# First layer's output projections in three terms for 14 of 16 tiles, one modulation group moved, VectorE's order changed in the first layer

## The chip, the cores and the metric

The kernel runs on one core of a Trainium2 chip. The metric is the device time of one execution in microseconds (us). TensorE multiplies matrices, VectorE and ScalarE do elementwise work, GpSimd (POOL) does masks and some transfers, SyncE (SP) issues most of the weight loads.

## The reference, cut to what matters

Two models of two layers each run one after the other on 256 tokens of width 1024. Only the first layer of the first model is touched by the change:

```python
cond = jax.nn.silu(c)
mod = cond @ ada_w[l] + ada_b[l]
shift, scale, gate = jnp.split(mod, 3, axis=-1)
h = rms_norm(x, norm_g[l]) * (1.0 + scale[:, None, :]) + shift[:, None, :]
z = h @ even_w_in[j]
a_val, a_glu, a_gate, r, k, v, wd, ad, b_gate = split_cols(z, EVEN_SIZES)
ya = conformer_conv(a_val, a_glu, conv_w[j], conv_vec[j]) * jax.nn.silu(a_gate)
yb = rwkv7_mix(r, k, v, wd, ad, ...).astype(h.dtype)
yb = yb * jax.nn.silu(b_gate)
out = jnp.concatenate([ya, yb], axis=-1) @ even_w_out[j]
x = x + gate[:, None, :] * out
```

`conformer_conv` is a causal convolution of 31 taps per channel with a layer norm; `rwkv7_mix` is a recurrence over heads of 64 channels with a norm per head. All is float32.

## The kernel before, in words

The activations lie transposed: 8 tiles (KT) of 128 channels by 256 tokens. Each engine has one hand-written program, and its order is the order of the code; engines wait for each other on counting semaphores. A queue of loads on SP fills a ring of weight slots, each as soon as its last reader is done (`place`, and L2486 where SP waits).

**The head.** The modulation `mod` is made in groups of 512 columns. `ada(c, half)` on VectorE multiplies four weight rows by `cond` and adds them up (L3152, L3156); `ada(c)` on TensorE sums over the partitions with one-column matmuls (L2605). The first four groups are made before hT, the normed input, can be scaled (L3200) and shifted by ScalarE (L2958). TensorE fills its waits with `keep_busy`, matmuls of ones whose result is not used (L2597). `AUX` holds constants for ScalarE's evictions.

**The projections of the first layer.** `z` (L2620) makes one tile of 128 output channels: eight float32 matmuls of 256 columns, one for each k. The trace has two records for each float32 matmul. VectorE takes keys, receptances and values with `lerp` (L3205) after ScalarE has thinned them (L2971). The keys' stage ends with L3275 and L3277, whose semaphore rwkv_set lets TensorE make head pairs (`lt_pair`, L2641).

**Masks and taps.** The convolution's 248 taps (`conv(n)`, L3226) are handed out on VectorE between other work. In the second half of the tokens they stand beside `kar_masks` and `br_masks` (L3325), which take head products from banks 2 and 3 so that TensorE can write the next pair there (`br_pair`, L2685). `states` then runs four steps of the recurrence.

**The output projections.** `eoA` are 8 tiles that multiply YY, the convolution branch, and `eoB` 8 tiles that multiply YT, the recurrence branch. VectorE adds each tile times the gate into xT (`out`, L3423). eoA tiles alternate between two banks: tile q waits for the sum of tile q-2. eoB uses four banks and begins when all eoA tiles are summed. Between the eoA tiles lies the norm over heads of YT: its sums and spreads on TensorE (L2457, L2467), squares and root on ScalarE (L3121, L3123), centring (L3441), reciprocal and scaling (L3450) on VectorE, gain and bias on ScalarE (L3126), then bonus and gate on VectorE (L3454, L3455). Behind eoB comes the second layer's norm (index 1), whose squares ScalarE makes as tiles are summed. VectorE also makes `ada(10)` between the halves and `ada(11)` after the norm, and the angle tables between the eoB sums.

The second layer's q projections (L746, code in `pe_rest`) already work in three terms: ScalarE copies a weight chunk of 256 columns in fp32r (`hb_r`, L1379), VectorE writes the rest, weight minus copy, over the chunk in the ring (L1753), and TensorE adds high times high, high times low and low times high.

## Time and profile before

| what | us |
|---|---|
| median of 3 runs | 2012.23 (2012.07 to 2014.06) |
| the profiled execution | 2008.93 |
| its span | 2007.2 |
| TensorE matmuls busy in the span | 1940.4 (97%) |
| VectorE busy | 1432.8 (71%) |
| ScalarE busy | 997.0 (50%) |

The profiled execution is one of its own, 3.3 us under the median. The rows below are from it. A row of the timeline has its start and its length in us, the engine, the line of the kernel, what it writes and reads, how many records it merges, and in brackets how long the engine was idle before it and what released it. Lengths of merged rows run from the first start to the last end.

### The profile page before, as it was taken

Reading aid. Unit: us, or ns where it says so; the run is one execution under the profiler, and the core shown is the slowest. Engines: PE = TensorE matmul, PEld = TensorE weight load, DVE = VectorE, ACT = ScalarE, POOL = GpSimd, SP = SyncE. Lnnn points to the kernel's source line nnn. Section 1 sums busy time; section 2 is a strip of 40 time slices with the busy share of each in tenths; the row PEclk is TensorE's granted clock in tenths of the full one; section 3 lists DMA queues with packets and bytes.
Section 4 is the critical chain, followed back from the end, with each engine's and each line's share of the span. In section 5 each row is a group of like instructions: output and inputs, shape, how many; then the busy total and the mean of one; then the engine's idle time right before and its main releaser. Section 6 shows DMA issues by size and latency. Waiting matters only on the chain.

```text
span 2007.2 us, 30019 instructions
## 1 busy us (share of the span) xinstructions
PE 1940.4 (97%) x12623; PEld 1763.6 (88%) x12623; DVE 1432.8 (71%) x1732; ACT 997.0 (50%) x1146; POOL 77.0 (4%) x122
## 2 busy tenths in 40 slices
PE   6999989999999999999999999999999999999997
PEld 5888878888888968999999898989898989898986
DVE  6688996464765346666545588888888888888873
ACT  2411111325465313433445566776677667776754
POOL 4010000000000100100220000000000000000000
PEclk9999999999999999999999999999999999999998
DMA  9845221443422432456663479999999999999971
GB/s 340 272 130 188 88 80 43 168 169 126 165 87 86 169 126 85 127 188 202 184 208 121 167 256 352 359 338 344 353 355 343 346 349 360 335 352 350 357 300 43
DMA packets 225857, 452.29 MB, mean 225 GB/s; under 512 B 6944, under 2 KB 91176, under 8 KB 225720
## 3 DMA queue, kind: packets, MB, share of 16 engines
q1 hardware_dynamic: 222128, 444.39, 63.1%
q0 software_dynamic: 1904, 5.80, 1.0%
q8 instruction: 102, 1.67, 0.3%
q10 hardware_dynamic: 1688, 0.15, 0.1%
q14 instruction: 35, 0.29, 0.0%
HBM read 448.21 MB, written 2.10 MB: 224 GB/s over the span
## 4 chain that ended last, share of the span: by engine, by line
PE 87%; DVE 8%; ACT 3%; issue 1%; DMA 1%; ACTq 0%; POOL 0%; DVEq 0%; POOLq 0%
PE bank L1208 25%; PE bank L1234 12%; PE bank L2620 8%; PE bank L957 6%; PE bank L2388 5%; PE bank L992 3%; PE bank L1040 2%; PE bank L840 2%; PE bank L881 2%; PE bank L758 2%; PE bank L1316 2%; PE bank L746 1%; DVE arena L3226 1%; PE bank L2357 1%; PE bank L1219 1%
## 5 line engine op out<-in xcount | busy, mean ns | idle before, releaser
L2120 DVE TENSOR_TENSOR ring_r<-ring,his_r 128x2816 fp32r<-128x2816 f32 (+1 forms) x192 | 587.2, 3085 | 42.8 <-ACT his_r L1626 42.3
L1626 ACT ACTIVATE his_r<-ring 128x2816 fp32r<-128x2816 f32 (+1 forms) x192 | 491.3, 2561 | 191.5 <-DMA ring<-in_moe_w_dram 183.6
L1208 PE MATMUL bank<-his_r,hg_r 128*128 128x352 f32 x2048 | 353.4, 324 | 0.0
L1208 PEld LDWEIGHTS bank<-his_r,hg_r 128*128 128x128 f32 x2048 | 332.0, 188 | 0.6
L2620 PE MATMUL bank<-hT,ring 128*128 128x256 f32 x912 | 209.4, 386 | 1.0 <-DVE arena L3205 0.5
L2620 PEld LDWEIGHTS bank<-hT,ring 128*128 128x128 f32 x912 | 171.6, 192 | 28.4 <-issue 5.1
L1208 PE MATMUL bank<-ring_r,hg_r 128*128 128x352 f32 x1024 | 186.2, 324 | 0.0
L1208 PEld LDWEIGHTS bank<-ring_r,hg_r 128*128 128x128 f32 x1024 | 169.2, 189 | 0.0
L3226 DVE SCALAR_TENSOR_TENSOR arena<-ring,cw,arena 128x256 f32<-128x256 f32 x240 | 96.5, 477 | 0.1
L1234 PE MATMUL bank<-his_r,at_hi_r 128*128 128x512 f32 x352 | 93.0, 397 | 0.0
L1234 PE MATMUL bank<-his_r,at_lo_r 128*128 128x512 f32 x352 | 92.5, 396 | 0.0
L1234 PE MATMUL bank<-ring_r,at_hi_r 128*128 128x512 f32 x352 | 92.4, 395 | 0.0
L957 PE MATMUL bank<-h_r,ffn_r 128*128 128x256 f32 x672 | 84.0, 283 | 0.0
L957 PEld LDWEIGHTS bank<-h_r,ffn_r 128*128 128x128 f32 x672 | 82.2, 192 | 0.0
L1234 PEld LDWEIGHTS bank<-ring_r,at_hi_r 128*128 128x128 f32 x352 | 66.1, 188 | 16.0
L1234 PEld LDWEIGHTS bank<-his_r,at_lo_r 128*128 128x128 f32 x352 | 66.1, 188 | 16.0
L1234 PEld LDWEIGHTS bank<-his_r,at_hi_r 128*128 128x128 f32 x352 | 64.9, 188 | 13.9
L3156 DVE SCALAR_TENSOR_TENSOR arena<-ring,cond,arena 128x512 f32<-128x512 f32 x84 | 63.1, 751 | 5.5 <-DMA ring<-in_ada_w_dram 2.5
L758 PE MATMUL bank<-hT,ring 128*128 128x256 f32 x256 | 58.5, 382 | 2.7 <-ACT arena L1421 2.7
L2388 PE MATMUL bank<-hT,ring 128*128 128x256 f32 x272 | 60.0, 380 | 1.0 <-ACT hT L2958 0.5
L2388 PEld LDWEIGHTS bank<-hT,ring 128*128 128x128 f32 x272 | 51.4, 190 | 9.3 <-issue 1.6
L2227 DVE TENSOR_TENSOR at_lo_r<-bank,at_hi_r 128x512 fp32r<-128x512 f32 (+1 forms) x48 | 29.5, 642 | 40.8 <-ACT at_hi_r L1686 40.6
(564 smaller groups left out, 3015.5 us busy)
## 6 DMA issues: line engine op xcount, KB each, us to landing
ring<-in_moe_w_dram SPq DMA_DIRECT2D x128, 1408.0 KB, 8.5
ring<-in_moe_w_dram SPq DMA_DIRECT2D x48, 1536.0 KB, 8.7
ring<-in_even_w_in_dram SPq DMA_DIRECT2D x28, 1024.0 KB, 6.6
ring<-in_ffn_w_dram SPq DMA_DIRECT2D x22, 1024.0 KB, 5.3
ring<-in_ada_w_dram SPq DMA_DIRECT2D x20, 1024.0 KB, 10.2
ring<-in_odd_w_in_dram SPq DMA_DIRECT2D x9, 2048.0 KB, 7.8
ring<-in_moe_w_dram SPq DMA_DIRECT2D x16, 1024.0 KB, 7.0
ring<-in_a_w_in_dram SPq DMA_DIRECT2D x6, 2048.0 KB, 7.9
```

Source lines behind the costliest of these rows:

```text
L758: ins = mm(bank[3][:, 0:T], w[:, k, (q % 4) * P:(q % 4 + 1) * P], h(k), start=(k == 0), stop=(k == KT - 1))
L840: ins = mm(bank[q % 4][:, 0:T], w[:, k, :], gt_r[x][:, k, :], start=(w is hi and x == 0 and k == 0), stop=(x == 1 and k == 2 * KT - 1))
L957: ins = mm(bank[first + m][:, 0:T], w[:, k, m * P:m * P + P], h_r[:, x, k, :], start=(w is hi and x == 0 and k == 0), stop=(w is lo and k ...
L992: ins = mm(bank[j % 4][:, 0:T], w[:, k, :], x[:, k, :], start=(w is hi and x is fa_hi_r and k == 0), stop=(w is lo and k == FT - 1))
L1208: ins = mm(bank[first + m][:, 0:WC], x[:, KT // 2 * late + k, :], w[:, k, WC * m:WC * m + WC], start=(not late and k == 0 and s == "hg_hi" ...
L1234: ins = mm(bank[2 * (e % 2) + half][:, :], x[:, f, :], y[:, m, 512 * half:512 * half + 512], start=(f == 0 and s == "at_hi"), stop=(f == F ...
L1626: A(moe_hi(n), moe_w(n), ACT.Copy).then_inc(sem("moe_hi"), 1)
L2120: V.tensor_tensor(moe_lo(n), moe_w(n), moe_hi(n).bitcast(F32), ALU.subtract).then_inc(sem("moe_lo"), 1)
L2388: mm = nc.tensor.matmul(bank[q % banks][0:width, 0:T], w[:, k, m * P:m * P + width], rhs(k), start=(k == 0), stop=(k == ph["k"] - 1))
L2620: ins = mm(z_bank(name, q), w[:, k, m * P:m * P + wide], rhs(k), start=(k == 0), stop=(k == KT - 1))
L3156: ins = V.scalar_tensor_tensor(acc, w[:, k, :], cond[:, m:m + 1], acc, ALU.mult, ALU.add)
L3226: V.scalar_tensor_tensor(YY[:, ct, :], UP[:, ct, j:j + T], cw[:, 8 * j + ct:8 * j + ct + 1], YY[:, ct, :], ALU.mult, ALU.add).then_inc(tap ...
```

## The change

It has seven parts.

1. eoA tiles 2 to 7 and all eoB tiles are made in three fp32r terms (`eo_terms`). A pair of tiles shares 256 columns of weights: ScalarE copies them (`eo_cast`) to one of three buffers, VectorE writes the low part over the ring (`eo_low`). YY is copied and split once (qh_r), YT in two halves (yb_r).
2. `ada(10)` moves from between eoA and eoB to behind the second layer's norm, ahead of `ada(11)`.
3. At the head `ada(3, 1)` goes ahead of the wait for the norm, the three AUX operations behind hT.
4. TensorE's parameter transposes go behind `ada(0)`; `keep_busy` has 14 matmuls instead of 22 there, and 8 instead of 24 ahead of the head pairs.
5. `ada(8, 0)` goes ahead of L3266, `receptance(2)` behind it.
6. Eight taps go from ahead of `br_masks(1, 0, 2)` to the row behind `br_masks(1, 2, 4)`.
7. Some transfers count on shared semaphores (bs_loaded, lt_stored and tt_stored are gone). The values waited for ask for the same transfers.

```diff
+        EO_BUF = [(h_r[:, 0], hb_r[0], hb_r[1])[n] for n in (0, 1, 2, 0, 1, 0, 1)]
+        EO_FREE = {3: 0, 4: 1, 5: 3, 6: 4}
...
-            norm(1, lambda q: took("eoB", q + 1))
+            for q in range(KT):
+                if q in (1, 3):
+                    eo_cast(5 + q // 2)
+                act.wait_ge(*took("eoB", q + 1))
+                square(1, q)
+            root(1)
...
             norm(1, lambda ct: gs[:, 8 + ct:9 + ct], shift=True)
+            ada(10, 0)
+            ada(10, 1)
             ada(11, 0)
...
             ada(0)
+            turn_params()
             ada(1)
             for q in range(KT):
                 norm_tile(0, q)
-            keep_busy(6, 22)
+            keep_busy(6, 14)
...
-            keep_busy(3, 24)
+            keep_busy(3, 8)
...
+            def eo_terms(b, q, n, x):
+
+                hi, lo, parts = EO_BUF[n], eo_pair(n, ring_r_flat), ("yb0", "yb1") if n >= 3 else ("yy",)
+                pe.wait_ge(sem("eo_hi"), EO_HI[n])
+                for w, y in ((hi, 0), (lo, 0), (hi, 1)):
+                    if w is lo:
+                        pe.wait_ge(sem("eo_lo"), EO_LO[n])
+                    for k in range(KT):
+                        if k % (KT // len(parts)) == 0 and w is hi:
+                            part = parts[k * len(parts) // KT]
+                            pe.wait_ge(sem("eo_lo" if y else "eo_hi"), (EO_LO if y else EO_HI)[part])
+                        ins = mm(b, w[:, k, (q % 2) * P:(q % 2 + 1) * P], x[:, y, k, :], start=(w is hi and y == 0 and k == 0),
+                                 stop=(y == 1 and k == KT - 1))
+                ins.then_inc(acc_ready, 1)
...
+            pe.wait_ge(*took("eoA", 8))
+            for q in range(KT):
+                if q >= 4:
+                    pe.wait_ge(*took("eoB", q - 3))
+                eo_terms(bank[q % 4][:, 0:T], q, 3 + q // 2, yb_r)
+                norm_behind(1, all_of=True)(q)
...
+            def eo_cast(n):
+                name, u = ("eoA", n + 1) if n < 3 else ("eoB", n - 3)
+                wait_chunk(act, name, u // 2, 0)
+                if n in EO_FREE:
+                    act.wait_ge(acc_ready, eo_done(EO_FREE[n]))
+                A(EO_BUF[n], eo_pair(n), ACT.Copy).then_inc(sem("eo_hi"), 1)
+
+            eo_cast(0)
+            eo_cast(1)
+            act.wait_ge(sem("conv_gated"), KT)
+            A(qh_r[:, 0, :, :], YY[:, :, :], ACT.Copy).then_inc(sem("eo_hi"), 1)
...
+            eo_cast(2)
...
+            eo_cast(3)
...
+            for g in range(2):
+                act.wait_ge(sem("yb_ready"), g + 1)
+                A(yb_r[:, 0, 4 * g:4 * g + 4, :], YT[:, 4 * g:4 * g + 4, :], ACT.Copy).then_inc(sem("eo_hi"), 1)
+                eo_cast(4 + g) if g == 0 else None
...
             for q in range(KT):
                 out("eoB", q, bank[q % 4][:, 0:T])
+                if q in (1, 3):
+                    eo_low(5 + q // 2)
                 if 1 <= q < 7:
                     angles(q - 1)
```

VectorE in the keys' stage, before: L3205 takes receptance tiles, L3266 the products of the decays, L3269 the scaling of the keys, L3152 and L3156 the modulation's group 8.

```order
L3261 RECIPROCAL nr<-nr 128x256
L3205 SCALAR_TENSOR_TENSOR arena<-bank,pc,arena 128x255 x2
L3266 TENSOR_TENSOR arena<-arena 128x2048
L3269 SCALAR_TENSOR_TENSOR arena<-arena,pc,bank 128x256 x8
L3152 TENSOR_SCALAR arena<-ring,cond 128x512
L3156 SCALAR_TENSOR_TENSOR arena<-ring,cond,arena 128x512 x3
L3205 SCALAR_TENSOR_TENSOR arena<-bank,pc,arena 128x255
```

The same stretch in the change (the lines stand 67 or 68 further down: L3333 is the old L3266, L3337 the old L3269):

```order
L3328 RECIPROCAL nr<-nr 128x256
L3272 SCALAR_TENSOR_TENSOR arena<-bank,pc,arena 128x255
L3219 TENSOR_SCALAR arena<-ring,cond 128x512
L3223 SCALAR_TENSOR_TENSOR arena<-ring,cond,arena 128x512 x3
L3333 TENSOR_TENSOR arena<-arena 128x2048
L3272 SCALAR_TENSOR_TENSOR arena<-bank,pc,arena 128x255
L3337 SCALAR_TENSOR_TENSOR arena<-arena,pc,bank 128x256 x8
L3272 SCALAR_TENSOR_TENSOR arena<-bank,pc,arena 128x255
```

The modulation's four operations have moved ahead of the decay products, and one of the two receptance tiles behind them.

VectorE beside the masks of the second half of the tokens, before: L3226 are taps, L3325 the masks (br), L3336 the first sum of the state.

```order
L3226 SCALAR_TENSOR_TENSOR arena<-ring,cw,arena 128x256 x12
L3325 TENSOR_TENSOR arena<-bank,bmask 128x4x128 x2
L3226 SCALAR_TENSOR_TENSOR arena<-ring,cw,arena 128x256 x8
L3325 TENSOR_TENSOR arena<-bank,bmask 128x4x128 x2
L3226 SCALAR_TENSOR_TENSOR arena<-ring,cw,arena 128x256 x30
L3336 TENSOR_TENSOR arena<-bank,arena 32x8x64 x2
```

In the change:

```order
L3293 SCALAR_TENSOR_TENSOR arena<-ring,cw,arena 128x256 x4
L3392 TENSOR_TENSOR arena<-bank,bmask 128x4x128 x2
L3293 SCALAR_TENSOR_TENSOR arena<-ring,cw,arena 128x256 x8
L3392 TENSOR_TENSOR arena<-bank,bmask 128x4x128 x2
L3293 SCALAR_TENSOR_TENSOR arena<-ring,cw,arena 128x256 x38
L3403 TENSOR_TENSOR arena<-bank,arena 32x8x64 x2
```

Eight taps have moved from ahead of the first masks to behind the last ones; their sum is the same.

VectorE in the eoA projections, before: L3423 sums a tile into xT, L3441 centres, L3450 scales, L3454 and L3455 add the bonus and gate.

```order
L3423 SCALAR_TENSOR_TENSOR xT<-bank,mod,xT 128x256 x2
L3441 SCALAR_TENSOR_TENSOR arena<-bank,arena 128x512 x4
L3423 SCALAR_TENSOR_TENSOR xT<-bank,mod,xT 128x256 x2
L3445 RECIPROCAL nr<-nr 128x256
L3423 SCALAR_TENSOR_TENSOR xT<-bank,mod,xT 128x256
L3450 TENSOR_TENSOR arena<-arena,bank 128x512 x4
L3454 TENSOR_TENSOR arena<-arena 128x1024
L3455 TENSOR_TENSOR arena<-arena 128x1024
L3423 SCALAR_TENSOR_TENSOR xT<-bank,mod,xT 128x256
```

The same work in the change, up to the scaling (L3527; L3490 is the old L3423, L3504 the low part of a pair, L3508 that of YY):

```order
L3490 SCALAR_TENSOR_TENSOR xT<-bank,mod,xT 128x256
L3508 TENSOR_TENSOR qh_r<-arena,qh_r 128x2048
L3504 TENSOR_TENSOR ring_r<-ring,h_r 128x8x256
L3490 SCALAR_TENSOR_TENSOR xT<-bank,mod,xT 128x256
L3515 SCALAR_TENSOR_TENSOR arena<-bank,arena 128x512 x4
L3504 TENSOR_TENSOR ring_r<-ring,hb_r 128x8x256
L3490 SCALAR_TENSOR_TENSOR xT<-bank,mod,xT 128x256 x2
L3520 RECIPROCAL nr<-nr 128x256
L3504 TENSOR_TENSOR ring_r<-ring,hb_r 128x8x256
L3490 SCALAR_TENSOR_TENSOR xT<-bank,mod,xT 128x256
L3504 TENSOR_TENSOR ring_r<-ring,h_r 128x8x256
L3527 TENSOR_TENSOR arena<-arena,bank 128x512 x4
```

Five low parts of 2048 columns stand between the sums and the norm's steps where none stood before; low parts of YT's halves follow behind each half's gate.

## Rows read from the trace of the kernel before

**Rows 1.** The page's chain that ended last, by engine.

```profile
PE 87%; DVE 8%; ACT 3%; issue 1%; DMA 1%; ACTq 0%; POOL 0%; DVEq 0%; POOLq 0%
```

**Rows 2.** Timeline of VectorE and TensorE at the head: start, length, idle before.

```profile
32.29 1.74 DVE L3194 RECIPROCAL nr<-nr 128x256 f32<-128x256 f32 x1
34.06 3.11 DVE L3156 SCALAR_TENSOR_TENSOR arena<-ring,cond,arena 128x512 f32<-128x512 f32 x4
38.39 0.17 DVE L3166 TENSOR_TENSOR mod<-bank,pc 128x16 f32<-128x16 f32 x1 [1.22 <-PE bank L2605]
...
40.18 14.05 PE L2620 MATMUL bank<-hT,ring 128*128 128x256 f32 x64 [0.45 <-ACT hT L2958]
```

**Rows 3.** Timeline of VectorE, then TensorE, in the keys' stage.

```profile
98.33 0.48 DVE L3205 SCALAR_TENSOR_TENSOR arena<-bank,pc,arena 128x255 f32<-128x255 f32 x1 [3.48 <-ACT arena L2971]
98.73 2.28 DVE L3266 TENSOR_TENSOR arena<-arena 128x2048 f32<-128x2048 f32 x1
100.93 3.22 DVE L3269 SCALAR_TENSOR_TENSOR arena<-arena,pc,bank 128x256 f32<-128x256 f32 x8
...
104.58 2.33 DVE L3156 SCALAR_TENSOR_TENSOR arena<-ring,cond,arena 128x512 f32<-128x512 f32 x3
...
105.56 5.52 PE L2597 MATMUL bank<-ones,ident 128*128 128x128 f32 x48
111.88 2.06 PE L2641 MATMUL bank<-arena 64*128 64x128 f32 x32 [0.80 <-DVE arena L3277]
```

**Rows 4.** Timeline of VectorE, and TensorE's row at 300.99, at the masks.

```profile
294.91 4.83 DVE L3226 SCALAR_TENSOR_TENSOR arena<-ring,cw,arena 128x256 f32<-128x256 f32 x12
299.65 1.28 DVE L3325 TENSOR_TENSOR arena<-bank,bmask 128x512 f32<-128x512 f32 x2
...
300.99 1.16 PE L2685 MATMUL bank<-arena 64*128 64x128 f32 x16 [2.23 <-DVE arena L3325]
...
319.63 1.28 DVE L3336 TENSOR_TENSOR arena<-bank,arena 32x512 f32<-32x512 f32 x2 [2.46 <-PE bank L2728]
```

**Rows 5.** Timeline of TensorE, VectorE and ScalarE in the output projections.

```profile
398.53 10.63 PE L2620 MATMUL bank<-arena,ring 128*128 128x256 f32 x48
409.73 10.63 PE L2388 MATMUL bank<-arena,ring 128*128 128x256 f32 x48 [0.58 <-DVE xT L3423]
...
385.83 2.48 DVE L3441 SCALAR_TENSOR_TENSOR arena<-bank,arena 128x512 f32<-128x512 f32 x4 [0.62 <-PE bank L2467]
...
401.50 1.22 DVE L3454 TENSOR_TENSOR arena<-arena 128x1024 f32<-128x1024 f32 x1 [0.35 <-ACT arena L3126]
...
399.39 4.04 ACT L3126 ACTIVATE arena<-arena,pc 128x256 f32<-128x256 f32 x8 [5.07 <-DVE arena L3450]
```

**Rows 6.** Timeline of TensorE in two q tiles, and one low part on VectorE.

```profile
521.32 2.08 PE L746 MATMUL bank<-qh_r,hb_r 128*128 128x256 f32 x16
...
524.18 2.08 PE L746 MATMUL bank<-qh_r,hb_r 128*128 128x256 f32 x16
...
483.28 2.28 DVE L1753 TENSOR_TENSOR ring_r<-ring,hb_r 128x2048 fp32r<-128x2048 f32 x1
```

**Rows 7.** Windows of 2 us (last: granted clock, DMA share, GB/s); TensorE's row at 616.85.

```profile
64.00:66.00 2.00, 2.00 (x9) 1.61 (x8) 2.00 (x5) 1.79 (x5) 0.00 (x0) 0.70 1.08 375
...
70.00:72.00 2.00, 2.00 (x7) 1.62 (x6) 0.00 (x0) 0.00 (x0) 0.00 (x0) 0.59 0.93 340
...
616.00:618.00 2.00, 1.15 (x7) 1.10 (x8) 1.69 (x4) 1.97 (x6) 0.00 (x0) 0.94 0.00 0
...
620.00:622.00 2.00, 2.00 (x8) 1.65 (x7) 1.32 (x3) 0.00 (x0) 0.00 (x0) 0.70 0.00 0
...
616.85 0.66 PE L797 MATMUL bank<-ident,arena 128*128 128x128 f32 x4 [2.18 <-DVE arena L1851]
```

**Rows 8.** Timeline of ScalarE's first q cast and TensorE's first q tile.

```profile
459.41 1.90 ACT L1379 ACTIVATE hb_r<-ring 128x2048 fp32r<-128x2048 f32 x1
...
476.79 3.76 PE L746 MATMUL bank<-qh_r,hb_r 128*128 128x256 f32 x16
```

More of the change, by code:

```diff
@@ L533, in c_done, with eo_pair, eo_done @@
             return phases["cin"]["t0"] + 2 * u + 2
+        EO_BUF = [(h_r[:, 0], hb_r[0], hb_r[1])[n] for n in (0, 1, 2, 0, 1, 0, 1)]
+        EO_FREE = {3: 0, 4: 1, 5: 3, 6: 4}
+        EO_HI = {n: v for v, n in enumerate((0, 1, "yy", 2, 3, "yb0", 4, "yb1", 5, 6), 1)}
+        EO_LO = {n: v for v, n in enumerate(("yy", 0, 1, 2, 3, "yb0", "yb1", 4, 5, 6), 1)}
+        def eo_pair(n, flat=ring_flat):
+            name, u = ("eoA", n + 1) if n < 3 else ("eoB", n - 3)
+            return view(phases[name], u // 2, flat)[:, :, T * (u % 2):T * (u % 2) + T]
+        def eo_done(n):
+            name, u = ("eoA", n + 1) if n < 3 else ("eoB", n - 3)
+            return phases[name]["t0"] + 2 * u + 2
         OO_HI = ["x0", "x1", "x2", "w0", "x3", "w1", "x4", "x5", "x6", "x7"] + [f"w{q}" for q in range(2, 8)]
@@ L1349, in pe_rest, with act_rest @@
             ins.then_inc(sem("router_ready"), 1)
-        def act_rest(act, ch, A, norm, square, root, shifted):
-            norm(1, lambda q: took("eoB", q + 1))
+        def act_rest(act, ch, A, norm, square, root, shifted, eo_cast):
+            for q in range(KT):
[4 more added lines that the diff above has]
+            root(1)
             shifted(1)
@@ L2867, in _ @@
             states(1, lambda n, m: z("zA", 2 * n + m))
-            def eo(q):
-                z("eoA", q, lambda k: YY[:, k, :], (lambda k: (sem("conv_gated"), k + 1)) if q == 0 else None)
+            def eo_terms(b, q, n, x):
[11 more added lines that the diff above has]
+                ins.then_inc(acc_ready, 1)
+            def eo(q):
+                if q >= 2:
+                    pe.wait_ge(*took("eoA", q - 1))
+                    eo_terms(z_bank("eoA", q), q, q // 2 - 1, qh_r)
+                else:
+                    z("eoA", q, lambda k: YY[:, k, :], (lambda k: (sem("conv_gated"), k + 1)) if q == 0 else None)
             eo(0)
@@ L2882, in _ @@
                 eo(q)
-            pe_gemm("eoB", lambda k: YT[:, k, :], [took("eoA", 8)], ready=lambda k: (sem("yb_ready"), k // 4 + 1), between=norm_behind(1, all_of=True))
+            pe.wait_ge(*took("eoA", 8))
[4 more added lines that the diff above has]
+                norm_behind(1, all_of=True)(q)
             keep_busy(6, 13)
@@ L3200, in _ @@
                 V.scalar_tensor_tensor(hT[:, ct, :], xT[:, ct, :], gs[:, ct:ct + 1], nr[:, :], ALU.mult, ALU.mult).then_inc(sem("h_scaled"), 1)
+            ch(V.tensor_scalar(AUX[:, 0:24], pc[:, VEC["mu_r"]:VEC["mu_r"] + 24], -1.0, 1.0, ALU.mult, ALU.add))
+            ch(V.tensor_scalar(AUX[:, 24:32], cols8("k_a"), -1.0, 1.0, ALU.mult, ALU.add))
+            V.tensor_scalar(AUX[:, 32:33], mulora, -1.0, 1.0, ALU.mult, ALU.add).then_inc(sem("aux_ready"), 1)
             def lerp(n, name, q, dst, mu):
@@ L3262, in _ @@
             receptance(1)
-            receptance(2)
+            ada(8, 0)
             dve.wait_ge(sem("lora_taken"), 16)
@@ L3266, in _ @@
             V.tensor_tensor(XG[:, :, :], X2[:, :, :], X3[:, :, :], ALU.mult).then_inc(sem("grown"), 1)
+            receptance(2)
             dve.wait_ge(sem("spread_ready"), 1)
```

55 lines of the change are left out of this document (32 added, 23 removed).

## The prediction

> **What bounds the kernel now.** I read the chain of waits first: TensorE holds 87% of it and VectorE 8% [rows 1]. So an edit counts only where TensorE runs without a gap, or where TensorE waits for the engine that the edit relieves. The edits all lie before 480 us of the 2007.2 us span. Behind that no edit touches an instruction's work, and every engine starts from where the stage before left it, so I take a shift at 450 us to reach the end whole. The timelines then show four places. At the head TensorE's first projection starts at 40.18 us, and it waited for the chain VectorE, ScalarE that makes hT [rows 2]. At 111.88 us it waits 0.80 us for VectorE, behind 5.52 us of filler matmuls that do nothing else [rows 3]: with less filler the wait would be longer, so VectorE sets this point. At 300.99 us it waits 2.23 us for VectorE's masks [rows 4]. In the output projections TensorE is all but full: 0.58 us idle ahead of the second half at 409.73 us [rows 5].
>
> **The head (edit A).** The fourth modulation sum's second half (four products, 3.11 us, at 34.06) now runs ahead of the wait for the norm, and the three small AUX operations go behind hT. Before, the half sum ended at 37.17 us, TensorE turned it into a column (about 1.05 us), and the modulation began at 38.39 us after 1.22 us of waiting. Now the half sum starts when the row at 32.29 and its small neighbours did, at 31.9, and ends at 35.0; the reciprocal (1.74 us) runs while TensorE makes the column, so the modulation begins at 36.8 us. That is 1.6 us earlier, and hT and the projections' start at 40.18 move with it [rows 2]. AUX is wanted only when the first tile is done, over 3 us later, so it costs nothing. The weight chunk for the half sum is the one thing that might be late: the ring loads of that time need about 15 us, and this one was issued at about 14.8 us, which gives 30.2; I take it as there. The parameter transposes move between two column groups on TensorE and fill its wait there; VectorE is later than both, so no gain. **A = -1.6 us.**
>
> **The keys' stage (edit B).** Before, VectorE ran: key products (L3266, 2.28 us, from 98.73), eight head scalings (3.22), four products of the modulation (0.48 and 2.33), two further 2.3 us products, and released TensorE at 111.82 us [rows 3]. The change puts the four products (2.8 us) ahead, where VectorE idled 3.48 us for ScalarE from 94.85 to 98.33, and a receptance tile (0.48) behind L3266. So L3266 starts at 97.7, ends at 100.0, the tile ends at 100.4, the scalings at 103.6, the next tile at 104.0, and the two products at 108.6 us. Gain 3.2 us. TensorE must be there: its filler shrinks from 24 to 8 matmuls, 5.52 to 1.84 us, so it is free at 107.4 us and then waits about 1.2 us. The eight scalings need a spread that was ready at 98.6, and ScalarE's own work hangs on L3266, which comes earlier: neither holds. **B = -3.2 us.**
>
> **The masks (edit C).** Eight of the 12 taps (4.83 us for 12, so 0.4 each) go from ahead of the first pair of masks to the long row behind the second [rows 4]. The first masks begin 3.2 us earlier, at 296.5 us, and end at 297.8; TensorE is done with its tile at 298.7 and starts there instead of at 300.99. The wait of 2.23 us is gone and 0.9 us of slack is left. What is late next: the row of taps, now 38, ends at 317.2 us as before, since the sum of taps is the same; the state's first sum, which waited 2.46 us for TensorE until 319.63, would now be free at 317.4. So it just holds. TensorE has no other wait until 376 us. **C = -2.2 us.**
>
> **The output projections (edit D).** Durations are from the q projections, which already use three terms [rows 6]: a tile takes 524.18 - 521.32 = 2.86 us there, a low part by VectorE 2.28 us; a cast by ScalarE takes 1.9 us [rows 8]. A float32 tile takes 3.5 us (10.63 us for three [rows 5]). TensorE saves 0.64 us a tile. In the first half this does not reach the end, since tile 7 waits for tile 5's sum and the second half for tile 7's, and both stand on VectorE behind the added work. I followed it step by step with the old times as the origin. VectorE: sum of tile 0 until 380.5; ScalarE has made two casts and that of YY by 381.7; low part of YY 384.1, of pair 0 386.3; sum of tile 1 386.7; the four centrings (2.48) 389.1; low part of pair 1 391.3; sums of tiles 2 and 3 392.1; reciprocal 392.9 to 394.7; low part of pair 2 396.9; sum of tile 4 397.3; low part of pair 3 399.5; the four scalings (2.48) 401.9. ScalarE's eight gains (4.04) start at 400.1 instead of 399.39 [rows 5]; the first half of YT is added and gated (2 x 1.22) by 404.7, sum of tile 5 405.1, low part of YT's half (1.2) 407.1, second half of YT 409.5, sum of tile 6 409.9, cast and low part of it 411.9, sum of tile 7 412.2. TensorE: tile 6 done at 402.0, idle until 405.1, tile 7 done at 408.0, idle until 412.2. The second half begins 2.5 us later than at 409.73. VectorE is given 5 x 2.28 + 2 x 1.2 = 13.8 us here; most of it lies in its old idle time. In the second half TensorE's eight tiles save 8 x 0.64 = 5.1 us. Each later pair of casts and low parts takes about 4.4 us behind the tile that frees its buffer, and TensorE wants it 6.2 us behind it, so this holds with 1.8 us to spare. **D = +2.5 - 5.1 = -2.6 us.**
> The Trainium skill ("TensorE: Matmul & The Clock Gate", section "Back-to-back issue gap") gives N/2.4 + 2.5 ns as the gap, an estimate of 109 ns at 256 columns and 2.62 us for the 24 matmuls of a tile; this case's rows show 119 ns and 2.86 us [rows 6]. By the page the second half would be 1.9 us shorter still; the measured row decides, and I use 2.86.
>
> **The modulation group behind the next norm.** VectorE's eight products (6.0 us) go from 409.6 to 446.9 us, where the last group's eight began so far, which now begin 6.0 us later. Their reader on TensorE is at 473.9. Queued behind them are the last group, the low part of hT (then at 461.3) and q's first low part; TensorE wants these at 476.79 us [rows 8]. SP's load of the first q chunk into that group's slot goes from 440 to 453 us and lands at about 461; ScalarE's cast of it was at 459.4 and would be at 461, and TensorE's next demand is 476.79. Hidden, cost 0; if the load took 10 us more it would still be hidden.
>
> **The clock.** TensorE's granted clock is not in the code, and two edits leave holes. When TensorE had been idle 2.18 us at 616.85, the clock fell to half (1.2 of 2.4 GHz) at about 617.9 us and stayed there 3.4 us; from 64.6 to 71.4 us it was at half for 6.8 us [rows 7]. Half speed costs half that time where TensorE is the bound: 1.7 or 3.4 us. The gap of 2.23 us at 300.99 left it whole [rows 4]. The change has idle stretches of 3.1 and 4.2 us around tile 7, longer than either. At the head, with 14 instead of 22 filler matmuls (0.23 us each), TensorE has little but the one-column groups between 32 and 36 us. I take 1.7 us for each (the row with idle time before it is the nearer one), 0 and 3.4 as the ends. **Clock = +3.4 us (0 to +6.8).**
>
> **Sum.** -1.6 - 3.2 - 2.2 - 2.6 + 3.4 = -6.2 us. The profiled execution took 2008.93 us (span 2007.2 and 1.7 around it), so one like it gives 2002.7. The runs' median is 2012.23, 3.3 us above, which I put down to nothing I can see in one trace; that gap stays, and the forecast is 2012.23 - 6.2 = **2006.0 us**. 0.2% is 4.0 us, about what a measurement of this kernel can tell from no change.
>
> **Rivals.**
> *The clock does not fall in the holes.* For it: the gap at 300.99 left it whole. Against: these are longer. It gives -9.6: 2002.6 us.
> *The clock takes back the gain.* Both holes cost 3.4 us, as the 6.8 us stretch did, and the hole of 1.2 us at 107 us, followed by half-height matmuls, adds 1.7. For: the filler is cut at both places where it stood between thin work. It gives -9.6 + 6.8 + 1.7 = -1.1: 2011.1 us.
> *Slower: pairs of weights become the bound.* In the second half, cast, low part and the next tile pair are a ring through three engines with two buffers. If the low part starts over 1.8 us later than worked out (VectorE has the angle tables and sums between), TensorE waits at tiles 2, 4 and 6. A full serial pass costs 4.4 us in place of overlap, so 3 x 3.5 = 10.5 us, with a half-speed stretch of 1.7 more than taken: -6.2 + 12.2 = +6.0, 2018.2 us. Against: the q tiles at 521 and 524 us ran through the same kind of ring without a gap between them [rows 6].
> *The change does nothing* (each saved stretch refilled by the next wait): 2012 us. Against: TensorE has no gap from 301 to 376 us to absorb it.
>
> **How the numbers follow.** Forecast 0.55; no fall of the clock 0.17; the clock takes it back 0.18; slower 0.05; nothing 0.05. The low end is the no-fall case less about 1 us for rounded steps, 2001.5; the high end the clock's case with 0.4 us for the same, 2011.5; outside are the slower case, nothing, and the tails. Faster by over 0.2% (under 2008.2): 0.17 and 0.51 of the forecast's 0.55, 0.68. Within: the other 0.04, the clock's 0.18 and nothing's 0.05, 0.27. Slower: 0.05.
>
> **What would show it.** Right: the first projection at 38.6 us; TensorE's first head pair at about 107 us (111.88 less 4.8, plus a clock stretch); no wait ahead of the second mask pair; tiles of 2.86 us in the output projections; TensorE idle twice around tile 7, about 3 and 4 us; the second half lasting about 5 us less, plus the clock's stretch. Wrong: a full clock through both holes, TensorE waiting at tiles 2, 4 or 6 for ring_r, or a q matmul that waits for a load.

## The result, and the profile after

| | before | changed |
|---|---|---|
| median, us | 2012.15 (2009.64 to 2014.06, 4 runs) | 1997.72 (1994.57 to 1998.2, 4 runs) |
| profiled execution, us | 2008.93 | 1994.57 |
| its span, us | 2007.2 | 1992.8 |

The ratio is 0.9926, with a 95% interval of 0.9909 to 0.9943. The forecast was 2006.0 us, in a range of 2001.5 to 2011.5 us: the sign was right, and the time lies 3.8 us below the range. All medians in this document are of fast runs: one run each of before (2719.71 us), of the changed kernel (10915.43 us) and of e7 (2158.92 us) lies far above all others and is left out.

The page of the changed kernel begins as that of before did: TensorE is full, and the chain that ended last is its own [rows 1].

```profile
PE 1924.8 (97%) x12687; PEld 1755.4 (88%) x12687; DVE 1452.1 (73%) x1742; ACT 1013.4 (51%) x1156; POOL 76.9 (4%) x122
...
PE 86%; DVE 8%; ACT 3%; issue 1%; DMA 1%; SPq 0%; POOL 0%; ACTq 0%; DVEq 0%; POOLq 0%
```

VectorE's busy time grew by 19 us and TensorE's fell by 16. The sum was made by stages, so I read the same four places.

**Head**, timeline of TensorE, then VectorE, then TensorE again, of the changed kernel [rows 2]:

```profile
18.82 1.84 PE L2630 MATMUL bank<-ones,arena 128*128 128x1 f32 x8
20.52 0.45 PE L2612 MATMUL bank<-ident,arena 128*128 128x128 f32 x1
...
21.26 0.48 DVE L3219 TENSOR_SCALAR arena<-ring,cond 128x512 f32<-128x512 f32 x1
...
33.26 1.75 DVE L3259 RECIPROCAL nr<-nr 128x256 f32<-128x256 f32 x1
35.04 0.17 DVE L3233 TENSOR_TENSOR mod<-bank,pc 128x16 f32<-128x16 f32 x1
...
36.83 1.53 PE L2645 MATMUL bank<-hT,ring 128*128 128x256 f32 x6 [0.93 <-ACT hT L3008]
```

The first projection starts at 36.83 instead of 40.18 us. The modulation (35.04) follows the reciprocal with no wait, where it had waited 1.22 us. The rows at 18.82 and 21.26 are the part that the prediction missed; they are read below.

**Keys' stage and masks**, VectorE and TensorE of the changed kernel [rows 3, 4]:

```profile
90.85 2.29 DVE L3333 TENSOR_TENSOR arena<-arena 128x2048 f32<-128x2048 f32 x1
...
98.88 1.95 PE L2622 MATMUL bank<-ones,ident 128*128 128x128 f32 x16
101.63 1.61 PE L2666 MATMUL bank<-arena 64*128 64x128 f32 x24 [0.80 <-DVE arena L3344]
...
286.26 1.28 DVE L3392 TENSOR_TENSOR arena<-bank,bmask 128x512 f32<-128x512 f32 x2
...
288.46 1.16 PE L2710 MATMUL bank<-arena 64*128 64x128 f32 x16
...
307.10 1.28 DVE L3403 TENSOR_TENSOR arena<-bank,arena 32x512 f32<-32x512 f32 x2
```

The first head pair comes at 101.63 instead of 111.88 us. TensorE's wait of 2.23 us at the masks is gone, and the state's first sum (307.10), which had waited 2.46 us for TensorE, follows the taps with no wait.

**Output projections**, TensorE, then VectorE of the changed kernel [rows 5]:

```profile
388.99 1.10 PE L2906 MATMUL bank<-qh_r,hb_r 128*128 128x256 f32 x8
392.79 2.07 PE L2906 MATMUL bank<-qh_r,hb_r 128*128 128x256 f32 x8 [2.69 <-DVE xT L3490]
394.66 1.91 PE L2906 MATMUL bank<-qh_r,ring_r 128*128 128x256 f32 x8
396.36 1.91 PE L2906 MATMUL bank<-qh_r,hb_r 128*128 128x256 f32 x8
399.88 1.22 PE L2906 MATMUL bank<-yb_r,h_r 128*128 128x256 f32 x8 [1.61 <-DVE xT L3490]
...
392.25 0.48 DVE L3490 SCALAR_TENSOR_TENSOR xT<-bank,mod,xT 128x256 f32<-128x256 f32 x1
...
399.35 0.48 DVE L3490 SCALAR_TENSOR_TENSOR xT<-bank,mod,xT 128x256 f32<-128x256 f32 x1
```

TensorE is idle for 2.69 us ahead of tile 7 and for 1.61 us ahead of the second half, each time until a sum on VectorE. Tile 7 ran at half speed: eight matmuls take 1.91 us there, and 1.10 us at 388.99. At 2.86 us for the tile the second hole would have been 4.2 us (399.88 - 392.79 - 2.86). The windows of 2 us of this stretch have the granted clock as the third number from the right (0.50 is 1.2 of 2.4 GHz); the first line is the place where before was at 0.70 [rows 7]:

```profile
64.00:66.00 2.00, 2.00 (x11) 1.77 (x10) 1.89 (x4) 0.00 (x0) 0.00 (x0) 1.00 1.06 393
...
392.00:394.00 2.00, 1.22 (x5) 1.22 (x6) 1.27 (x3) 1.63 (x2) 0.00 (x0) 0.52 0.00 0
396.00:398.00 2.00, 2.00 (x11) 1.98 (x10) 1.48 (x2) 0.89 (x1) 0.62 (x2) 0.50 0.00 0
400.00:402.00 2.00, 2.00 (x17) 2.00 (x18) 2.00 (x1) 0.00 (x0) 0.00 (x0) 1.00 0.84 111
```

The clock did fall in the hole, as forecast, but it cost nothing in this execution: it was back when the second half began, and tile 7's end was covered by VectorE, whose sum ended at 399.8 us. And the half-speed stretch that before had from 64 to 72 us is missing.

### The profile page after: what moved, and what is told of

Same layout as the page of the kernel before. It is cut to its first block, busy times and chain, and to the rows that moved or that the text cites. A ratio compares the mean times of both kernels' runs of the same rounds, so it can differ in the third digit from the quotient of the medians.

```text
span 1992.8 us, 30177 instructions
## 1 busy us (share of the span) xinstructions
PE 1924.8 (97%) x12687; PEld 1755.4 (88%) x12687; DVE 1452.1 (73%) x1742; ACT 1013.4 (51%) x1156; POOL 76.9 (4%) x122
## 4 chain that ended last, share of the span: by engine, by line
PE 86%; DVE 8%; ACT 3%; issue 1%; DMA 1%; SPq 0%; POOL 0%; ACTq 0%; DVEq 0%; POOLq 0%
PE bank L1224 25%; PE bank L1250 12%; PE bank L2645 8%; PE bank L973 6%; PE bank L2411 4%; PE bank L1008 3%; PE bank L1056 2%; PE bank L856 2%; PE bank L897 2%; PE bank L774 2%; PE bank L1332 2%; PE bank L2906 1%; PE bank L762 1%; PE bank L2380 1%; PE bank L1235 1%
```

## One table for all kernels

Each row is one profiled execution. It has TensorE's start in us at four marks (first projection, first head pair, first output tile, first tile of the next layer), what lies between the last two, and the stretches ahead of the last mark in which the granted clock was at half.

| kernel | first proj. | head pair | output | next layer | output stage | half speed at |
|---|---|---|---|---|---|---|
| before | 40.18 | 111.88 | 376.35 | 444.92 | 68.57 | 64-72 |
| before, second profile (e9) | 39.80 | 109.66 | 378.69 | 447.27 | 68.58 | 22-26, 36-43, 193-200, 302-306 |
| transposes alone (e1) | 38.03 | 106.40 | 374.05 | 442.63 | 68.58 | 191-196, 297-301 |
| whole head (e2) | 36.92 | 105.77 | 370.25 | 438.83 | 68.58 | 34-38 |
| keys alone (e3) | 40.73 | 105.58 | 373.24 | 441.81 | 68.57 | 37-41, 191-195, 296-301 |
| masks alone (e4) | 40.30 | 111.99 | 374.18 | 442.76 | 68.58 | 64-72 |
| without the terms (e5) | 36.95 | 104.52 | 368.25 | 436.82 | 68.57 | 22-26, 35-43, 189-193 |
| changed | 36.83 | 101.63 | 363.81 | 430.26 | 66.45 | 392-399 |
| changed, second profile (e6) | 36.92 | 101.97 | 364.15 | 433.24 | 69.09 | 34-38, 392-396, 399-407 |
| changed, 22 fillers (e11) | 37.04 | 101.83 | 365.56 | 433.53 | 67.97 | 22-27, 186-191, 394-399, 401-406 |
| sum sooner (e7) | 36.58 | 105.32 | 367.50 | 434.11 | 66.61 | 34-38, 61-69, 399-407 |
| other banks (e8) | 36.66 | 105.42 | 367.59 | 431.32 | 63.73 | 34-38, 61-69, 399-404 |
| hole filled (e10) | 36.86 | 101.66 | 365.44 | 427.76 | 62.32 | 22-26, 186-190 |
| second half only (e12) | 37.23 | 102.17 | 364.35 | 431.38 | 67.03 | 34-38 |

Whole-kernel times of one kernel scatter by up to 10 us, and this table shows one reason: the half-speed stretches lie elsewhere in each execution. A difference between two marks with no stretch between them repeats to 0.1 us.

## The experiments

The theory going in was: the edits took 11.2 us off TensorE's path (head 3.35, keys 3.45, masks 2.3, output stage 2.1), and the other 3 us of the profiled difference is a half-speed stretch that happened in one execution and not in the other. The rivals were the prediction's own step (the transposes give nothing), and that the change itself removes the stretch.

### e1: the transposes alone

```diff
-            <the four parameter transposes>
             ada(0)
+            turn_params()
             ada(1)
```

> The kernel before, with one thing changed: the four parameter transposes on TensorE stand behind the first column group instead of ahead of it. In the profile of before VectorE waited 1.87 us at 23.08 us for that column group, and the transposes had waited 1.55 us for their load. Theory (the transposes' place was on the path): VectorE's wait goes, the head's chain moves by about 1.75 us, the first projection starts at about 38.4 instead of 40.18 us, and the span falls by 1.8 us, or by 5.2 us if the half-speed stretch from 64 to 72 us goes too. Rival (the record's step, VectorE is later than both): no move, first projection at 40.2 us, span as before.

Measured: 2008.04 us against 2010.54 us, ratio 0.9987 (0.9974 to 0.9999). The marks say it more sharply. VectorE's second half sum, then TensorE's first projection, in this kernel:

```profile
21.18 0.48 DVE L3155 TENSOR_SCALAR arena<-ring,cond 128x512 f32<-128x512 f32 x1
...
38.03 3.26 PE L2622 MATMUL bank<-hT,ring 128*128 128x256 f32 x14 [0.45 <-ACT hT L2961]
```

The wait of 1.87 us is gone and the first projection comes 2.15 us sooner. The transposes' place was on the path; the prediction's step falls. How much it is worth depends on the execution. These are the same rows of before in its second profile (e9), VectorE first:

```profile
21.82 0.49 DVE L3152 TENSOR_SCALAR arena<-ring,cond 128x512 f32<-128x512 f32 x1 [0.51 <-PE bank L2605]
...
20.75 1.85 PE L2605 MATMUL bank<-ones,arena 128*128 128x1 f32 x16
```

TensorE's 16 one-column records took 1.85 us there and 3.42 us in the first profile, although the granted clock reads 1.00 from 20 to 22 us in both, and VectorE waited 0.51 instead of 1.87 us. Against e9 the edit brings VectorE's row 0.64 us forward (21.82 to 21.18); the other 1.1 of the 1.77 us at the first projection are e9's half-speed stretch from 36 us on. e3 and e4, in which these instructions are as in before, have the row at 22.99 and 23.20 us: three of four executions are like the first. The stretch at 64 us is missing in e1, and two short ones at 191 and 297 us gave that gain back, so it is not a property of the kernel.

### e2: the whole head

> The kernel before with the whole head edit (transposes moved, second half of the fourth modulation sum ahead of the wait for the norm, AUX behind hT, 14 filler matmuls instead of 22). Theory: -3.35 us, the first projection at 36.8 us, of which the transposes give 1.75 and the half sum 1.6; if the missing half-speed stretch at 64 to 72 us follows from the head's edit, 3.4 us more, -6.8 us in all. Rival (record): -1.6 us, first projection at 38.6 us. Second rival for the clock: the stretch comes and goes between runs of one kernel, then this profile may show it at another place and the several runs' mean clocks scatter by 0.002.

The edit is parts 3 and 4 of the change, but for the filler ahead of the head pairs. Measured: 2005.39 us, ratio 0.9976 (0.9965 to 0.9988). The first projection starts at 36.92 us, 3.26 us sooner: the theory's 3.35, not the prediction's 1.6. Of this 1.1 us come with the half sum and the thinner filler (38.03 in e1 to 36.92). The half-speed stretch sits at 34 to 38 us and costs 0.5 us (68.85 us from first projection to head pair, 68.37 in e1), because TensorE has nothing on the path there until 36.9 us.

### e3: the keys' stage alone

```diff
             receptance(1)
-            receptance(2)
+            ada(8, 0)
             ...  (XG)
+            receptance(2)
             ...  (spread)
-            ada(8, 0)
-            keep_busy(3, 24)
+            keep_busy(3, 8)
```

> The kernel before with the keys' stage alone edited (four products of the modulation ahead of the wait, one receptance tile behind the product, filler 24 to 8). Both theories: TensorE's first head pair 3.2 to 3.5 us earlier than at 111.88 us, and the span 3.2 to 3.5 us shorter; the half-speed stretch at 64 to 72 us stays, since nothing ahead of it is touched. If the stretch is gone here too, it isn't the head's doing.

Measured: 2005.39 us, ratio 0.9976 (0.9965 to 0.9988). From first projection to head pair it takes 64.85 us. Before took 71.70 us with a stretch worth 3.4 in it and e1, which had none there, 68.37 us. So the edit is worth 3.5 us. The stretch at 64 us is missing here as well, although nothing ahead of it was changed: it isn't the head's doing.

### e4: the taps alone

```diff
-            conv(12)
+            conv(4)
             br_masks(1, 0, 2)
             conv(8)
             br_masks(1, 2, 4)
-            conv(30)
+            conv(38)
```

> The kernel before with the taps alone re-ordered (4, 8, 38 instead of 12, 8, 30). Both theories: TensorE's wait of 2.23 us at 300.99 us goes and the span is 2.2 us shorter. Rival: the tap row of 38 or the state's first sum takes it back behind 307 us, then the stage after it, at 376.35 us, is not earlier.

Measured: 2005.91 us, ratio 0.9982 (0.9972 to 0.9991). The second mask pair starts with no wait, and head pair to first output tile takes 262.19 instead of 264.47 us: 2.3 us, kept to the end of the stage.

```profile
298.82 1.16 PE L2685 MATMUL bank<-arena 64*128 64x128 f32 x16
```

### e5 and e6: everything but the terms, and the changed kernel again

e5 is before with the edits of e2, e3 and e4 together: the output projections stay in float32 and `ada(10)` in its old place. e6 is the changed kernel without an edit.

> The kernel before with edits A, B and C, that is, the changed kernel without the three-term output projections and with the modulation group in its old place. Marks on TensorE against before: first projection -3.3 us, first head pair -6.7 us plus whatever a half-speed stretch adds or takes (-10.1 where the one at 64 to 72 us is missing), first output tile 2.3 us more. Theory (D is worth 2.1 us on the path): this kernel is 2.1 us longer than the changed one at the start of the next stage (at 444.92 us in before), stretches of half speed set aside. Rival (D loses at tile 7 what it saves): no difference there.

> The changed kernel itself, timed in as many rounds as the experiments. Theory: the edits take 11.2 us off TensorE's path (3.35, 3.45, 2.3, 2.1), and the rest of the 14.4 us is in how many half-speed stretches a run happens to have, which differ between runs of one kernel: with many runs the difference of the medians lies near 11 us. Rival: the change itself removes a half-speed stretch of 3.4 us, then it stays at 14 to 15 us.

Measured: e5 2000.98 us, ratio 0.9949 (0.9935 to 0.9964); the changed kernel 1997.9 us, ratio 0.9935 (0.9918 to 0.9952), 11.8 us under the median of before in the same series, 2009.72 us. The output stage takes 68.57 us in e5, and 66.45, 69.09 and 67.97 us in the three profiles with the changed kernel's order (changed, e6, e11). The first of them is free of the clock, which gives the edit 2.1 us. The other two had another half-speed stretch on the start of the second half. TensorE's row there, and a window, in e6:

```profile
400.21 2.07 PE L2906 MATMUL bank<-yb_r,h_r 128*128 128x256 f32 x8 [2.71 <-DVE xT L3490]
...
404.00:406.00 2.00, 2.00 (x11) 2.00 (x11) 0.26 (x1) 0.00 (x0) 0.00 (x0) 0.50 1.04 412
```

That is a cost of 0, 2.6 and 1.5 us, 1.4 on the mean: of the 2.1 us that the edit gives on the path, the clock took 1.4 on the mean of these three profiles.

### e7 and e8: the sums sooner, other banks

```diff
+            out_a(5)
             for g in range(2):
                 ...  (add the bonus, gate)
-                out_a(5 + g)
-                ...  (low part of this half of YT)
+            out_a(6)
+            for g in range(2):
+                ...  (low part of this half of YT)
```

and for e8 also

```diff
-            pe.wait_ge(*took("eoA", 8))
+            pe.wait_ge(*took("eoA", 7))
             for q in range(KT):
+                if q == 3:
+                    pe.wait_ge(*took("eoA", 8))
...
-                eo_terms(bank[q % 4][:, 0:T], q, 3 + q // 2, yb_r)
+                eo_terms(bank[(q + 1) % 4][:, 0:T], q, 3 + q // 2, yb_r)
```

(VectorE's sums of the second half read the banks one further on too.)

> The changed kernel with VectorE's order around tile 7 changed: the sum of tile 5 ahead of YT's first addition, both halves of YT added and gated before the sum of tile 6, then both low parts. Worked out from the changed kernel's durations: tile 7 starts at 390.0 instead of 392.79 us, TensorE's hole of 2.69 us shrinks to about 0.2, and the second half still waits for the sum of tile 7, at 398.2 instead of 399.88 us: -1.5 us. If the holes of TensorE are what makes the clock fall at 392 us, the half-speed stretch stays, since the time idle only moves behind tile 7 (about 5 us there).

> The same, and the second half's tiles in the banks one further on (1, 2, 3, 0), so that its first tile needs the sum of tile 6 alone and starts while tile 7's sum is still open. Worked out: second half from 395.8 us instead of 399.88 us, hole between about 2.9 us: -4.1 us against the changed kernel, -2 if the low part of the next pair (from 398.2 to 400.5 us) becomes late for the tile behind.

e7: 1998.57 us, ratio 0.9934 (0.9918 to 0.9951), no gain over the changed kernel's 1997.9. Tile 7 has no hole in front now; the idle time lies behind it, in one piece:

```profile
401.56 2.07 PE L2906 MATMUL bank<-yb_r,h_r 128*128 128x256 f32 x8 [4.83 <-DVE xT L3490]
```

Counted from the first output tile the second half starts at 34.06 us instead of 36.07, 2.0 us sooner, but then runs at half speed up to 407 us, and the stage takes 66.61 us as against 66.45. The expectation of -1.5 us missed: it left out that the clock's fall would land on the second half.

e8: 1994.03 us (1993.6 to 1995.66), ratio 0.9914 (0.9898 to 0.993), 3.9 us under the changed kernel, whose runs in the same series went from 1997.17 to 1999.52 us. The expectation was 4.1. TensorE's rows and a window:

```profile
398.97 0.74 PE L2906 MATMUL bank<-yb_r,h_r 128*128 128x256 f32 x4 [2.13 <-DVE xT L3492]
400.02 1.22 PE L2906 MATMUL bank<-yb_r,h_r 128*128 128x256 f32 x4 [0.31 <-ACT yb_r L3194]
...
400.00:402.00 2.00, 1.98 (x9) 1.99 (x10) 2.00 (x4) 0.00 (x0) 1.35 (x2) 0.50 1.05 410
```

### e9: before again

> The kernel before itself, profiled a second time. Theory (half-speed stretches come and go between runs of one kernel): some of the stretches of its first profile (64 to 72, 474 to 482, 617 to 622, 1959 to 1967 us) are at other places or missing, and the marks between them move by 1.7 or 3.4 us, above all at 111.88 us. Rival (each kernel has its own fixed stretches): the one at 64 to 72 us is there again and 111.88 us is hit within 0.3 us.

Measured: 2008.07 us (2006.3 to 2014.31) against 2009.62 us for the same kernel, ratio 0.9992 (0.9982 to 1.0003). The stretch at 64 us is gone and others have come. The one from 36 us began behind 2.18 us in which TensorE had been idle (until 35.72 us). A window at the old place, and one of 7 us at a new one:

```profile
64.00:66.00 2.00, 2.00 (x11) 1.74 (x10) 2.00 (x5) 1.45 (x4) 0.00 (x0) 1.00 0.78 242
...
36.00:43.00 7.00, 7.00 (x27) 6.37 (x28) 3.77 (x11) 3.30 (x8) 0.00 (x0) 0.51 1.06 376
```

The theory holds and its rival (each kernel has its own stretches) falls: same code, and 111.88 us became 109.66, 444.92 became 447.27. The stretch comes back elsewhere too: e4 has it at 64 to 72 us, and e7 and e8, whose head is that of the change, have one at 61 to 69 us. So the change doesn't remove it either.

### e10: the hole filled

```diff
+            keep_busy(6, 9)
             pe.wait_ge(*took("eoA", 7))
```

> The kernel with the other banks, and nine filler matmuls (2.1 us) on TensorE behind tile 7, where it was idle for 2.13 us before the second half. Theory (the idle time makes the clock fall): the stretch of 3.42 us at 399 us is gone, the second half is 1.7 us shorter, -1.7 us against the version without filler. Rival (the stretch comes whatever TensorE does there): it stays, time as before or up to 0.3 us more, if the last filler ends behind the sum.

Measured: 1993.03 us (1990.77 to 1997.45), ratio 0.9917 (0.9903 to 0.9931), the lowest median of all, though against e8's 1994.03 us the runs don't tell them apart, and their mean granted clocks are alike (0.9915 and 0.9914). What the filler did is seen in the profile alone. TensorE's filler, the second half, and a window:

```profile
394.52 2.17 PE L2622 MATMUL bank<-ones,ident 128*128 128x128 f32 x18
396.81 0.74 PE L2906 MATMUL bank<-yb_r,h_r 128*128 128x256 f32 x4
397.86 0.74 PE L2906 MATMUL bank<-yb_r,h_r 128*128 128x256 f32 x4 [0.31 <-ACT yb_r L3195]
...
400.00:402.00 2.00, 2.00 (x19) 2.00 (x18) 2.00 (x2) 0.00 (x0) 0.00 (x0) 1.00 1.14 238
```

The clock is whole through the stage, which takes 62.32 us, 1.4 less than e8 and 6.3 less than before. Five profiles with a hole of over 2 us around tile 7 (changed, e6, e7, e8, e11) all had a stretch of half speed between 392 and 407 us, and the one with the hole filled had none. e12, with a hole of 3.31 us ahead of the second half, had none either, so a hole makes the fall likely and not certain. The seven profiles of kernels with the old stage (before, e9, e1 to e5) have no such hole there and no stretch between their marks for the output and the next layer.

### e11: the head's filler back

> The changed kernel with 22 filler matmuls at the head instead of 14. Three of the five kernels with 14 showed a half-speed stretch of 3.4 us at 34 to 38 us, just ahead of the first projection. Theory (the thinner filler lets the clock fall, as the prediction supposed): no stretch there with 22, and the filler of 1.84 us more ends before VectorE is ready or delays the first projection by under 0.5 us. Rival: the stretch at 34 us shows here too, or the first projection comes 1 to 2 us later because the column groups stand behind the filler.

The edit is 22 for 14 in the head's filler. Measured: 1997.76 us, ratio 0.9935 (0.9922 to 0.9948). The first projection starts at 37.04 us, 0.2 us later than in the changed kernel, and the stretch sits at 22 to 27 us. Over all profiles, kernels with 14 fillers had a stretch somewhere in 34 to 43 us in six of eight, kernels with 22 in two of six: too few to blame the filler. A stretch that ends at 38 us costs 0.1 to 0.7 us (first projections of 14.20 to 14.70 us where 14.05 is usual); the one to 43 us in e5 lay on the projections and cost 2.8 (67.57 us to the head pair, 64.80 in the changed kernel), and before's second profile had one like it.

### e12: three terms in the second half only

```diff
             def eo(q):
-                if q >= 2:
-                    ...  (eo_terms)
-                else:
-                    z("eoA", q, ...)
+                z("eoA", q, ...)
```

and the casts and low parts of YY and of the first three pairs are gone.

> The changed kernel with the first half of the output projections (six tiles) back in float32, only the second half in three terms. The prediction's sum: the first half's added work costs 2.5 us at the start of the second half, whose saving is 5.1 us. Theory: without the four low parts of the first half (9.1 us of VectorE) TensorE has no hole ahead of tile 7, the second half starts 2.3 to 3.0 us sooner than at 399.88 us, and the kernel is that much shorter than the changed one, and 3.4 us at most more where the changed one had a half-speed stretch in the second half. Rival (the three-term tiles of the first half pay): this kernel is 1 to 2 us longer than the changed one.

Measured: 1997.32 us (1995.49 to 2002.71), ratio 0.9942 (0.9927 to 0.9956), which the runs don't tell from the changed kernel. The output stage takes 67.03 us, 0.6 more than the changed kernel's. Tile 7's start and the second half on TensorE, and the sum that released it:

```profile
394.01 3.69 PE L2645 MATMUL bank<-arena,ring 128*128 128x256 f32 x16 [0.31 <-DVE xT L3481]
401.01 1.22 PE L2906 MATMUL bank<-yb_r,h_r 128*128 128x256 f32 x8 [3.31 <-DVE xT L3481]
...
400.48 0.48 DVE L3481 SCALAR_TENSOR_TENSOR xT<-bank,mod,xT 128x256 f32<-128x256 f32 x1
```

The second half starts 36.66 us after the first output tile, where the changed kernel took 36.07: not sooner, although VectorE was spared 9.1 us of low parts. The theory was wrong here, and the rival too high. VectorE's four scalings start 23.81 us after the first output tile in e12, 23.21 in the changed kernel and 22.31 in before: without low parts VectorE waited for the slower float32 tiles (2.97 and 1.46 us ahead of two sums) instead. From the scalings to the second half it takes 12.85 and 12.86 us, and 11.07 in before; that chain of YT (scale, gain, add, gate, cast, low part, sum) is the same in both. So three terms in the first half cost nothing at the start of the second, low parts and faster tiles taken together; what the low parts cost by themselves wasn't tried.

## Why the prediction was wrong, point by point

**The head, A: -1.6 us predicted, -3.3 us measured.** The half sum moved ahead gave 1.1 to 1.2 us (e1 against e2 and the changed kernel) where 1.6 was worked out; the other 2.15 us are the transposes (e1). In an execution like e9 they are worth 0.6. The step that failed is "The parameter transposes move between two column groups on TensorE and fill its wait there; VectorE is later than both, so no gain." VectorE was not later. These are rows of before that the prediction did not have, VectorE first, then TensorE:

```profile
23.08 0.49 DVE L3152 TENSOR_SCALAR arena<-ring,cond 128x512 f32<-128x512 f32 x1 [1.87 <-PE bank L2605]
...
20.36 0.48 PE L2588 MATMUL bank<-ident,arena 128*128 128x128 f32 x1 [1.55 <-DMA posi<-in_positions_dram]
...
21.25 3.42 PE L2605 MATMUL bank<-ones,arena 128*128 128x1 f32 x16
```

TensorE waited 1.55 us for a load of parameters, with the column group that VectorE needed to free its accumulator queued behind. I followed the chain back from 40.18 us to 31.9 us and called VectorE's order there the start; eight us further back stood a wait for TensorE of 1.87 us, with nothing but back-to-back work between. The chain had to be followed until it met something that no edit touches. That A was only 1.7 us short hides this: a term of 2.15 us had been put at nothing.

**The keys' stage, B: -3.2 predicted, -3.5 measured** (e3). TensorE's wait there is 0.80 us again, for the same engine, and VectorE's order is the one worked out.

**The masks, C: -2.2 predicted, -2.3 measured** (e4). No new wait appeared; the slack of the first sum of the state was enough.

**The output stage, D: -2.6 predicted, -2.1 measured** (changed against e5, clock aside). The tiles run 2.86 us apart, and the second half starts 2.7 us later, as forecast (2.5), and then gains 4.8 (5.1 forecast). VectorE's timetable held: from tile 7's start to the second half it is 7.09 us where 7.1 was worked out, and the holes are 2.69 us for 3.1, and 1.61 us for 4.2 only because tile 7 ran at half speed and filled the rest. What the list of added work left unclear is which part of it delays the second half: of the 2.7 us, 0.9 lie ahead of the four scalings and 1.8 behind them, where the casts and low parts of YT are (e12). Another order of VectorE's sums around tiles 5 to 7, with the banks one further on, takes more than that back: in e8 the second half starts 31.38 us after the first output tile instead of 36.07, with no work removed. The formula that the prediction quotes from the Trainium skill ("TensorE: Matmul & The Clock Gate", section "Back-to-back issue gap") is given there for a single matmul by itself, and the page says that it is off for a stream. The tiles here again ran 2.86 us apart.

**The modulation group: 0 predicted, 0 measured.** Between before and the changed kernel the start of the next layer differs by 14.66 us and the third q tile, behind the moved group, by 14.66 too (486.30 and 471.64 us); between e5, which has the group in its old place, and the changed kernel by 6.56 and 6.57 us. It wasn't tried alone.

**The clock: +3.4 us predicted, and this is the largest miss.** The term "I take 1.7 us for each" adds two falls to the base. At tile 7 the mechanism was right: the fall comes with the hole, and not in the profile whose hole is filled (e10), though e12's hole came without one. The cost was 0, 2.6 and 1.5 us in three profiles; that the mean of 1.4 is near 1.7 is luck, since two of the three had two stretches there. At the head the price was wrong: a stretch came there in six of eight profiles with the thinner filler, but five of the six cost 0.1 to 0.7 us, because half speed costs only where TensorE has work on the path; and it came with 22 fillers too (e3, e9). Nor does it come on top: the mean granted clock of the changed kernel is 0.9916 over nine runs, not below before's 0.9911 over 73.

**The base.** The forecast started from 2012.23 us, the median of three runs. Over the three series of experiments, e9's runs with them, before has a median of 2009.65 us (73 runs, 2005.38 to 2015.81), and the changed kernel 1997.77 (9 runs, the first four among them): 11.9 us, with 11.2 on the path. At one mean granted clock, 0.991, the means are 2009.22 us (30 runs) and 1998.24 us (5 runs), 11.0 apart. So most of the 3.3 us between the profile and its median, which the prediction could not explain, is a draw. The stretch at 64 to 72 us in the one profile of before is a draw too; that the profiled executions differ by 14.4 us, as the medians do, is chance.

So the sum by steps: -3.3 - 3.5 - 2.3 - 2.1 = -11.2 us on the path, where the forecast had -9.6; -0.7 left for the clock and all else, by difference and not measured by itself, where it had +3.4; and 2.5 us of the measured 14.4 are draws of the two sets of four runs. The rival in which the clock does not fall, 2002.6 us, was nearest in size and for the wrong reason: it fell.

**What stays open.** Mean times of e2, e3 and e4 lie 4.8 to 5.4 us under before's 2010.67 us in their series, where their marks give 3.3, 3.5 and 2.3 us; e5, with all three, is 8.7 us under by its median where the marks give 9.1. Part of this is scatter, and e4's mean clock is higher (0.9927 against 0.9910 for before). Whether an edit makes costly stretches rarer, and what decides that one falls on 64 us, one or two profiles of each kernel can't tell. Nor do they tell why TensorE's rows at 20 us take twice as long in most executions.

## What to carry to other kernels

Follow the waiting chain of an engine back until it ends in something that no edit can move, across all back-to-back rows: a load that another engine waits for at 20 us can be the start of a projection at 40 us. Before a sum is made against one profile, list its half-speed stretches and leave them out of the base, since they are draws; price the idle time that a change creates as a possible fall of the clock on the work behind it, and try work that nobody reads in it where a bank is free (in e10 the profiled stage became 1.4 us shorter, while the medians don't tell the kernels apart). When the accumulators' sums stand between two groups of tiles, the order of sums against other work, and which bank the next group begins in, can be worth more than the work saved: e8 gained 3.9 us over the changed kernel with another order of the sums and the banks one further on.

## What the runs showed of the hardware

- The clock falls to half also while TensorE is busy without a gap: in before at 64 us (TensorE busy 8.00 us of the 8 from 56 us on) and at 474 us (busy 8.00 us of the 8 from 466 us on). What ran just before were matmuls of one column and of 64 partitions at 64 us, and these at 474 us, with weights of 64 of 128 columns, then 8 columns and one column streamed:

```profile
466.67 3.67 PE L697 MATMUL bank<-hT,ring 128*64 128x256 f32 x32
470.27 3.74 PE L703 MATMUL bank<-ring,hT 128*128 128x8 f32 x32
473.87 3.06 PE L2605 MATMUL bank<-ones,arena 128*128 128x1 f32 x16
```

  The stretch of e9 from 36 us on isn't of this kind: 2.18 us of idle time stand ahead of it.
- All 14 profiled executions have a half-speed stretch of some 7 to 10 us that begins between 455 and 477 us. Of the places in the first 310 us (22, 34 to 43, 61 to 72, 186 to 200, 296 to 306 us) each execution but the first of the changed kernel shows some.
- A stretch of 7 us costs 3.3 us on the path (first projection to head pair: 71.70 us in before, 68.37 in e1), one of 3.4 us about 1.6 (e1: the lead of 5.48 us at 111.88 us fell to 3.89 behind the one at 191 us), and nothing where TensorE waits anyway.
- Executions of before with a mean granted clock of 0.988 took 2014.3 us on the mean (8 runs), those with 0.995 took 2006.1 us (3 runs). Not all of the scatter goes with it: the 30 runs at 0.991 lie between 2006.33 and 2013.14 us.
- A granted clock of 1.00 doesn't say that TensorE runs at its usual pace: 16 one-column records at 21 us took 3.42 us in before and 1.85 in e9, and both profiles have 1.00 up to 22 us.
- Tile by tile, three terms in fp32r took 2.86 us against 3.5 us in float32, in this stage as in the q projections [rows 6].
